# Masked logits kept in SBUF between the maximum and the exponential; four output weight rows rounded by GpSimd; new softmax step tables

## The reference, cut to what matters

```python
logits = einsum('bqhd,bqkhd->bqhk', q_b, k_sel) * att_scale
logits = where(valid, logits, -inf)            # 256 keys of each query, chosen by the indexer
p = softmax(logits, axis=-1)
o = einsum('bqhk,bqkhd->bqhd', p, v_sel)
...
y = concatenate([y_conv, y_attn], axis=-1) @ w_out
return x + gate * y
```

## Time and profile before

| what | value |
|---|---|
| three runs | 693.77, 696.41, 696.93 us |
| the profiled execution | 694.33 us |
| its span, first to last instruction | 692.5 us |
| attention, from the last exponential of head 0 to that of head 7 | 480.86 to 585.91, 105.05 us |
| mean granted TensorE clock | 0.998 of 2.4 GHz |

### The profile page before, as it was taken

How to read it: one execution, slowest core, us unless ns; L and a number is a source line. 1 busy time by engine, 2 the same in 40 slices (tenths; PEclk the granted TensorE clock), 3 DMA queues, 4 the chain that set the end, 5 groups by cost and what they waited for, 6 DMA issues and landing times.

```text
span 692.5 us, 8909 instructions
## 1 busy us (share of the span) xinstructions
PE 656.3 (95%) x3203; PEld 546.8 (79%) x3203; DVE 451.2 (65%) x750; ACT 377.8 (55%) x550; POOL 223.7 (32%) x117
## 2 busy tenths in 40 slices
PE   0899999999999999999999999999999999999996
PEld 0789987878888888888888887887878777778884
DVE  4884635667889999994059550004989898577635
ACT  6865445656661324452643545435989988874302
POOL 1001215343234243756845676340034422000000
PEclk9999999999999999999999999999999999999999
DMA  8960497353333010101110550162973440122431
GB/s 318 379 224 1 121 172 177 124 151 93 92 91 123 31 61 31 61 31 62 45 48 30 187 178 30 31 154 63 334 180 93 122 123 26 37 92 91 153 122 61
DMA packets 27910, 78.63 MB, mean 114 GB/s; under 512 B 3986, under 2 KB 8410, under 8 KB 27868
## 3 DMA queue, kind: packets, MB, share of 16 engines
q1 hardware_dynamic: 27524, 77.03, 37.2%
q10 hardware_dynamic: 344, 1.05, 0.6%
HBM read 61.25 MB, written 13.41 MB: 108 GB/s over the span
## 4 chain that ended last, share of the span: by engine, by line
PE 83%; DVE 4%; ACT 3%; SPq 3%; DMA 3%; issue 3%; POOL 1%; ACTq 0%; DVEq 0%; POOLq 0%
PE ps L795 17%; PE ps L797 17%; PE ps L796 17%; PE ps L999 4%; PE ps L1000 4%; PE ps L1001 4%; PE ps L827 3%; PE ps L859 3%; PE ps L860 2%; PE ps L879 2%; PE ps L878 2%; PE ps L947 2%; PE ps L946 2%; DMA raw<-in_w_units 2%; SPq L554 2%
## 5 line engine op out<-in xcount | busy, mean ns | idle before, releaser
L795 PE MATMUL ps<-hH,wH 128*128 128x512 f32 (+1 forms) x544 | 211.7, 389 | 1.6 <-issue 1.5
L796 PE MATMUL ps<-hL,wH 128*128 128x512 f32 (+1 forms) x544 | 210.1, 386 | 0.0
L797 PE MATMUL ps<-hH,wL 128*128 128x512 f32 (+1 forms) x544 | 210.1, 386 | 0.0
L1826 POOL TENSOR_TENSOR wL<-raw,wH 128x1024 fp32r<-128x1024 f32 x35 | 86.4, 2469 | 184.6 <-ACT wH L1053 176.2
L795 PEld LDWEIGHTS ps<-hH,wH 128*128 128x128 f32 x544 | 102.2, 188 | 21.8 <-issue 3.1
L797 PEld LDWEIGHTS ps<-hH,wL 128*128 128x128 f32 x544 | 102.1, 188 | 20.3
L796 PEld LDWEIGHTS ps<-hL,wH 128*128 128x128 f32 x544 | 102.2, 188 | 18.4
L1661 DVE CUSTOM_DVE_ANT_0 ps<-ps,bias 128x128 f32<-128x128 f32 (+3 forms) x64 | 48.7, 762 | 50.6 <-PE ps L860 50.4
L1254 ACT ACTIVATE relu<-ps,wabs 128x384 f32<-128x384 f32 (+5 forms) x48 | 40.0, 849 | 39.5 <-PE ps L879 17.2
L1668 DVE TENSOR_TENSOR phL<-ps,phH 128x512 fp32r<-128x512 f32 (+1 forms) x80 | 50.5, 635 | 13.0 <-ACT phH L1212 11.9
L1555 DVE SCALAR_TENSOR_TENSOR score<-relu,wsgn,score 128x384 f32<-128x384 f32 (+5 forms) x42 | 49.7, 1184 | 13.7 <-ACT relu L1254 10.8
(11 more groups left out here) (229 smaller groups left out, 1140.7 us busy)
## 6 DMA issues: line engine op xcount, KB each, us to landing
raw<-in_w_units SPq DMA_DIRECT2D x36, 512.0 KB, 3.4
ks<-qk_halves SPq DMA_DIRECT2D x32, 256.0 KB, 5.9
xin<-in_x SPq DMA_DIRECT2D x8, 512.0 KB, 8.1
wa<-in_w_ada SPq DMA_DIRECT2D x8, 512.0 KB, 11.9
wa<-in_w_ada SPq DMA_DIRECT2D x16, 256.0 KB, 7.5
gw<-in_w_ada SPq DMA_DIRECT2D x8, 512.0 KB, 4.2
qs<-qk_halves SPq DMA_DIRECT2D x16, 256.0 KB, 4.2
wo<-in_w_out SPq DMA_DIRECT2D x8, 512.0 KB, 9.3
```

The lines of the kernel that those rows point to most:

```text
L795: pe.matmul(out, wH[slot(n)][:, kt, :], hH[:, kt, cols], start=(kt == 0), stop=False)
L796: pe.matmul(out, wH[slot(n)][:, kt, :], hL[:, kt, cols], start=False, stop=False)
L797: mm = pe.matmul(out, wL[slot(n)][:, kt, :], hH[:, kt, cols], start=False, stop=(kt == KT - 1))
L1826: g.tensor_tensor(wL[slot(n)][:], raw[slot(n)][:], wH[slot(n)][:].bitcast(F32), ALU.subtract).then_inc(s_wL, 1)
```

## The change

Two SBUF tiles `masked` of 128 x 1024 f32 are added, at KB 56 and 60, which are the places of `wo` tiles 6 and 7. From head 1 on the maximum's pass writes the masked logits there instead of back to PSUM, and the exponential reads them there. PE's waits on `s_exp` for a free bank become waits on `s_mx`, the maximum. The maximum of u now waits for the exponential of u-2, which frees its tile.

The tiles `wo` 6 and 7 are loaded after the last exponential. Tiles 0 to 3 are rounded and split by POOL in `out_split`, two after the first pair and two after the second; ACT keeps tiles 4 to 7. The step tables are new.

```diff
-LOGITS_AT = (2, 5, 10, 13, 15, 16, 18, 20)
-MAX_AT = (1, 5, 9, 12, 14, 15, 17, 20)
-EXP_AT = (6, 9, 13, 14, 16, 18, 21, 23)
+LOGITS_AT = (1, 3, 10, 13, 14, 15, 16, 18)
+MAX_AT = (1, 2, 9, 14, 14, 15, 15, 18)
+EXP_AT = (9, 13, 13, 16, 16, 17, 19, 21)
...
-DSQ_AT = {HEAD * (2 * t + 1) + (4 if t < NT - 1 else 5): t for t in range(NT)}
-DENS_AT = {HEAD * (2 * t + 1) + (11 if t < NT - 1 else 7): t for t in range(NT)}
-KEEP_AT = {HEAD * (2 * t + 1) + (13 if t < NT - 1 else 9): t for t in range(NT)}
+DSQ_AT = {HEAD * (2 * t + 1) + (7 if t < NT - 1 else 5): t for t in range(NT)}
+DENS_AT = {HEAD * (2 * t + 1) + (13 if t < NT - 1 else 7): t for t in range(NT)}
+KEEP_AT = {HEAD * (2 * t + 1) + (14 if t < NT - 1 else 9): t for t in range(NT)}
...
-KEEP_SUMS_AT = {HEAD * (2 * t + 2) + 6 + 8 * half: (t, half) for t in range(NT - 1) for half in range(2)}
-OUT_HIGH_AT = {HEAD * (2 + ct) + 13: ct for ct in range(4)}
-OUT_HIGH_AT.update({LAST + x: 4 + n for n, x in enumerate((11, 14, 17, 18))})
+KEEP_SUMS_AT = {HEAD * (2 * t + 2) + 5 + 8 * half: (t, half) for t in range(NT - 1) for half in range(2)}
+OUT_HIGH_AT = {LAST + x: 4 + n for n, x in enumerate((11, 14, 17, 18))}
...
+        masked = [at(f"masked{i}", [P, S], F32, kb) for i, kb in enumerate((56, 60))]
...
+        def masked_of(u):
+            return logit_bank(u) if u < NB else masked[u % 2][:, 0:(u % NB + 1) * P]
...
-                    for ct in range(KT):
+                    for ct in range(KT - 2):
                         sp.dma_start(wo[:, ct, :], ...).then_inc(s_wo, 16)
...
+            sp.wait_ge(s_exp, NB * NH)
+            for ct in (KT - 2, KT - 1):
+                sp.dma_start(wo[:, ct, :], ...).then_inc(s_wo, 16)
...
                 elif bank == 3:
-                    pe.wait_ge(s_exp, NB * h + (7 if h else 8))
+                    if h:
+                        pe.wait_ge(s_mx, NB * h + 7)
+                    else:
+                        pe.wait_ge(s_exp, NB)
...
+                elif u == NB + 1:
+                    pe.wait_ge(s_exp, NB)
+                    pe.wait_ge(s_evac, NU)
                 elif u > NB:
-                    pe.wait_ge(s_exp, u - 1)
-                    if u == NB + 1:
-                        pe.wait_ge(s_evac, NU)
+                    pe.wait_ge(s_mx, u - 1)
...
-                A(prob_of(sb, i % 4), logit_bank(u), ACT.Exp, bias=nmx[:, u:u + 1], scale=-1.0,
+                A(prob_of(sb, i % 4), masked_of(u), ACT.Exp, bias=nmx[:, u:u + 1], scale=-1.0,
...
-                act.wait_ge(s_wo, 16 * KT)
                 if ct == 4:
+                    act.wait_ge(s_woL, NT)
                     act.wait_ge(s_lg, NB * NH)
                 if ct == 6:
+                    act.wait_ge(s_wo, 16 * KT)
...
-                src = logit_bank(u)
-                v.tensor_tensor_reduce(src, src, bias_of(i), -ATT_SCALE, ...)
+                if u == NB:
+                    dve.wait_ge(s_unit, NU)
+                elif u >= NB + 2:
+                    dve.wait_ge(s_exp, u - 1)
+                v.tensor_tensor_reduce(masked_of(u), logit_bank(u), bias_of(i), -ATT_SCALE, ...)
...
-            def out_low(ct):
+            def out_split(ct):
+                pool.wait_ge(s_wo, 16 * (KT - 2))
+                g.tensor_copy(wo_high(ct), wo[:, ct, :]).then_inc(s_woH, 1)
                 pool.wait_ge(s_woH, ct + 1)
...
-                if t:
-                    out_low(2 * t - 1)
                 pair_square(t, 1)
                 pair_gate(t, 1)
                 pair_add(t, 0)
                 pair_add(t, 1)
                 if t < 2:
-                    out_low(2 * t)
+                    out_split(2 * t)
+                    out_split(2 * t + 1)
```

More of the change, by code:

```diff
@@ L652, in _ @@
                     spread_den((h - 3) // 2)
+            sp.wait_ge(s_exp, NB * NH)
+            for ct in (KT - 2, KT - 1):
+                sp.dma_start(wo[:, ct, :], a["w_out"][P * ct:P * ct + P, :]).then_inc(s_wo, 16)
             sp.wait_ge(s_tp, last_chunk(2 * NH - 2) + 1)
@@ L820, in turn @@
                 elif bank == 3:
-                    pe.wait_ge(s_exp, NB * h + (7 if h else 8))
+                    if h:
+                        pe.wait_ge(s_mx, NB * h + 7)
+                    else:
+                        pe.wait_ge(s_exp, NB)
                 elif bank == 0:
-                    pe.wait_ge(s_exp, NB * NH)
+                    pe.wait_ge(s_mx, NB * NH)
                 for j in js:
@@ L959, in group_sums @@
                 if t < NT - 1:
-                    pe.wait_ge(s_exp, NB * (2 * t + 2) + 8)
+                    pe.wait_ge(s_mx, NB * (2 * t + 2) + 8)
                     if half:
@@ L978, in out_step @@
                     elif b == 0:
-                        pe.wait_ge(s_exp, NB * NH - 1)
+                        pe.wait_ge(s_mx, NB * NH - 1)
                     elif b == 1:
-                        pe.wait_ge(s_exp, NB * NH)
+                        pe.wait_ge(s_mx, NB * NH)
                         pe.wait_ge(s_pl, turned_into(0, NH - 1, range(2, 7)))
@@ L1659, in row_max @@
                 dve.wait_ge(s_lg, u + 1)
-                src = logit_bank(u)
-                v.tensor_tensor_reduce(src, src, bias_of(i), -ATT_SCALE, 3.0e38, ALU.add, ALU.min, nmx[:, u:u + 1]).then_inc(s_mx, 1)
+                if u == NB:
+                    dve.wait_ge(s_unit, NU)
+                elif u >= NB + 2:
+                    dve.wait_ge(s_exp, u - 1)
+                v.tensor_tensor_reduce(masked_of(u), logit_bank(u), bias_of(i), -ATT_SCALE, 3.0e38, ALU.add, ALU.min, nmx[:, u:u + 1]).then_inc(s_mx, 1)
             def low_prob(k):
```

## The result

The changed kernel takes 690.45 us, the median of nine runs (689.49 to 692.72), against 693.81 (693.37 to 697.24) for the kernel before on the same chip: a ratio of 0.9944, with a 95% interval of 0.9926 to 0.9961. That is 0.56% faster, a small gain, but the interval lies wholly under 1. The profiled execution has a span of 689.2 us (692.5 before) and took 691.02 with what lies around it.

A forecast was written before the change was run, and what follows sets the result against it. No single engine bounds the attention: each window is its busiest engine's work plus hand-over waits. Even windows 2.25, odd 1.8 and window 1's 0.5 us make 4.55; 696.41 - 4.55 = 691.8 us, range 686.5 to 697.5.

The forecast's parts named there:

- The bank freed by the maximum: Attention, windows of one head each: logits of u wait for the maximum of u-2, not its exponential; 0.5 us in windows 2 to 7.
- the certain wait: Block 1's logits waiting for block 7's exponential of the head before; odd windows lose 0.6 us each, 1.8 in all.
- the other waits on exponentials: Further waits on exponentials in the attention, at most 0.6 us each, said to go or shrink in the same way.
- The floor of the even windows: Attention windows 2, 4, 6: DVE's 13.35 us as floor, plus 0.45, makes 13.8 each, a gain of 2.25 us.
- the 0.7 us a window that I had found and priced for `dT`: Even windows: block 5's logits wait for `dT` behind block 4's maximum; PE loses about 0.7 us each, said to be affordable.
- The exponential from SBUF: ACT in the attention: 26 ns more for each of eight exponentials, 0.2 us a window, bounds 0 and 0.4.
- SP and the end: `wo` tiles 6 and 7, loaded behind the last exponential, arrive by about 595; counted as nothing, 1 to 2 us if uncovered.
- Window 1: First attention window: 14.79 us less 0.5, with at most 0.3 us off its gain for the start.
- Slower: Rival, 700.8 us, chance 0.12: maxima on DVE wait for the exponential of u-2 and hold up everything behind; 4.4 us more.
- Handed back: Rival, 695.8 us, chance 0.22: DVE's waits for exponentials (1.8 us) and PE's for `dT` take 3.9 of the 4.55 us.
- GpSimd holds VectorE: Rival, 694.9 us, chance 0.07: GpSimd's new work holds `dsq` in heads 3 and 5, 1.5 us each, 3.0 us.
- Full gain: Rival, 687.8 us, chance 0.14: every wait in the attention goes; windows sum to 96.4 against 105.05, a gain of 8.6.

## Why the prediction was right, and where it was not

**The time** was 691.8 forecast and 690.45 measured, and that they lie so near is in part luck. The forecast counted down from 696.41, a median of three runs; over nine runs the kernel before takes 693.81, so that the profiled 694.33 was not a quick one, and from there the forecast gain would have given 689.3. The gain itself was 4.55 us forecast, and 3.36 measured by medians. In the windows it is 4.14, or 3.6 without the moved mark, and it came this near by two errors of opposite sign and like size: 1.6 us too little for the odd windows, 2.15 too much for the even ones.

**The bank freed by the maximum** is the gain, as the prediction had it: 3.8 us, shown by putting the waits back. Its size per window was wrong for the odd ones. The step that failed is "15.56, 15.52 and 15.52, less the 0.6 us of the certain wait". The part on the freed bank has 0.5 us for this wait, and names the other waits on exponentials, which "go or shrink in the same way"; the sum puts them at nothing. Measured, the odd windows are 1.13 to 1.17 us shorter each. Two things were missed, both visible before. First, block 6's logits waited for block 4's exponential as well; in window 5 of the kernel before:

```profile
550.75 0.19 ACT L1204 ACTIVATION_READ_ACCUMULATOR prob<-ps,nmx 128x1 f32 x1
...
550.99 0.19 PEld L859 LDWEIGHTS ps<-ks,qs 128*128 128x128 f32 x1 [0.16 <-ACT prob L1204]
550.99 0.50 PE L859 MATMUL ps<-ks,qs 128*128 128x512 f32 x1
```

The view counts 0.16 us for the weight load and nothing for the matmul, so I let it go. How the 1.15 us divide among the waits, no run shows. Second, I read PE's 15.1 us of busy time as its own work. With 90 matmul rows in window 3 either way, PE is busy for 15.13 us in the run with the old waits and for 14.40 in the run with early `dT`: the matmul rows are as long in both, within 0.5% in sum, so 0.7 us of the busy column was the tail of matmuls behind which PE stood. I had used that very argument to call 0.37 us of idle time 0.5 of loss in the earlier trace rows, and not applied it to the column.

**The floor of the even windows** was the larger error: "PE can afford it in windows where DVE is the floor". The earlier trace rows spoke against it: PE's busy time in windows 2, 4 and 6, 13.67 to 13.73 us, stood above VectorE's 13.29 to 13.39, and the prediction passed it over. Nor was VectorE's 13.35 us a floor: with `dT` early window 4 takes 13.30, of which VectorE is busy for 12.76 and PE for 13.07. The run with only `dT` early settles it: the 0.7 us a window that I had found and priced for `dT` counted in full, and measured 0.86 a window (2.57 in three, from 100.91 to 98.34). Without that wait the even windows gain 2.7 us, against 2.25 forecast. The term was right, and the reason to drop it was not.

**Prices.** The exponential from SBUF: 26 ns forecast, 33 measured, inside the bounds. The Trainium skill, "VectorE: DVE Perf Modes", section on the TRN2 errata, gives ScalarE 224 cycles of fixed cost from SBUF against 172 from PSUM, an estimate of 43 ns at 1.2 GHz; the eight sizes show 25 to 41, so the sign agrees and the size is a little less. The maximum into SBUF: nothing forecast, nothing found. GpSimd's copy: 1.2 us forecast, 1.04 measured, and in head 3 its work ends at 526.99, before the 528.2 that I gave it. SP and the end: no instruction waits for tiles 6 and 7, as forecast. Window 1: 0.5 us forecast, 0.6 read, 0.1 without the moved mark.

**The rivals.** "Slower", by the maxima's new wait: that wait is not listed once. "Handed back": half of it is true, the `dT` wait at 2.6 us; VectorE's waits on exponentials, its other half, are nil. "GpSimd holds VectorE": the mechanism is shown, at 0.4 to 1.0 us instead of 1.5, but not in the changed kernel, where GpSimd is done first. The Trainium skill, "GPSIMD Engine Reference", section Key points, says that the two engines share SBUF interfaces and contend where a VectorE instruction has two SBUF inputs; the six `dsq` rows that end with a GpSimd subtraction agree. "Full gain", 8.6 us: the kernels with early `dT` come near its 687.8 us, at 687.80 to 688.80, but only because the forecast started too high. Their gain is 5.3 to 6.2 us by medians, and 6.3 to 6.8 in the windows with the moved mark, where the odd ones stop at PE's 14.4. The prediction's argument against this rival, that no window came closer than 0.8 us to its busiest engine, misread: in windows 3, 4, 5 and 7 PE's busy time is within 0.37 to 0.44 us of the window.

## What to carry to other kernels

A busy column is not an engine's own work: the same matmuls kept PE busy for 0.7 us less in a window once nothing held them up, so take a floor from a stretch in which the engine waits for nothing, or leave it open. And compare the columns of all engines before one is called the floor. When a new wait has been found and priced, count it, unless the engine that is to hide it has been shown to be late by itself. And when a buffer is freed earlier, look through the written order for small operations that others wait for and that now stand behind long ones: here one number in a table was worth over half of what the change had gained.

## What the hardware showed

A VectorE operation on 16 columns with two SBUF inputs, 0.17 us alone, was drawn out to 0.54 to 1.21 us six times, each time to the end of a running GpSimd subtraction, while the subtractions kept their 2.38 to 2.41 us. The readout behind the maximum took 139 ns where the maximum wrote to PSUM and about 84 where it wrote to SBUF; it overlaps the next instruction, and the kernel with the old waits, where the maximum writes to SBUF too, gains at most 0.14 us in windows 2 to 7. ScalarE pays 25 to 41 ns more for an exponential that reads SBUF and not PSUM.
